# Norms of query features and latents from compact sums, and latents stored by two engines

## The reference, cut to what matters

```
z = rmsnorm(x, g_norm) @ w_in;   cq (384), ckv_raw (256), kr (32), ... = split(z)
q    = rmsnorm(cq, g_q) @ w_uq
ckv  = rmsnorm(ckv_raw, g_kv)         # returned: kv_latent of prompt and sample
k_pe = rope(kr, pos)                  # returned: k_rope of prompt and sample
mk, mv = split(rmsnorm(mem, g_mem) @ w_mem_kv)   # returned: memory keys and values
rmsnorm(x, g) = x * rsqrt(mean(x*x, last axis) + 1e-6) * g
```

## Time and profile before

| | us |
|---|---|
| median of three runs (2205.89 to 2209.16) | 2206.71 |
| profiled execution, its time | 2208.78 |
| profiled execution, its span | 2207.0 |
| TensorE busy in the span | 1908.0 |
| VectorE busy in the span | 853.1 |
| ScalarE busy in the span | 610.6 |
| TensorE's mean granted clock | 0.937 |

### The profile page before, as it was taken

How to read it: one execution, slowest core, us unless ns; L and a number is a source line. 1 busy time by engine, 2 the same in 40 slices (tenths; PEclk the granted TensorE clock), 3 DMA queues, 4 the chain that set the end, 5 groups by cost and what they waited for, 6 DMA issues and landing times. The chain is left out here.

```text
span 2207.0 us, 31815 instructions
## 1 busy us (share of the span) xinstructions
PE 1908.0 (86%) x13375; PEld 1541.7 (70%) x13375; DVE 853.1 (39%) x1487; ACT 610.6 (28%) x1153; POOL 605.5 (27%) x436
## 2 busy tenths in 40 slices
PE   6997988979997769999698888888469996999798
PEld 4643555559995346666577777777369996999776
DVE  4043455570104324444614464645541115121242
ACT  3020433342112323333222333333332223222221
POOL 0000000022213047451456000000165445445430
PEclk9998999989997999999899999999689998999899
DMA  7002000001111247561227212120143332333322
GB/s 259 0 10 61 4 7 10 1 11 44 43 39 39 76 148 235 207 184 45 72 63 198 51 47 53 46 51 11 39 137 86 86 86 57 87 86 86 128 73 77
DMA packets 186265, 167.86 MB, mean 76 GB/s; under 512 B 47228, under 2 KB 157372, under 8 KB 185756
## 3 DMA queue, kind: packets, MB, share of 16 engines
q1 hardware_dynamic: 162988, 112.89, 17.6%
q0 software_dynamic: 20592, 52.63, 8.1%
q10 hardware_dynamic: 2560, 0.56, 0.1%
HBM read 150.33 MB, written 23.01 MB: 79 GB/s over the span
## 5 line engine op out<-in xcount | busy, mean ns | idle before, releaser
L2429 PE MATMUL ps<-activations_high,weights_high 128*128 128x272 f32 x1152 | 242.8, 292 | 55.2 <-ACTq L2415 28.9
L2429 PE MATMUL ps<-activations_high,weights_low 128*128 128x272 f32 x1152 | 239.6, 290 | 0.0
L2429 PEld LDWEIGHTS ps<-activations_high,weights_high 128*128 128x128 f32 x1152 | 182.9, 191 | 57.0 <-ACT weights_high L2245 29.1
L882 DVE TENSOR_SCALAR sb<-sb 128x1536 int32<-128x1536 int32 (+3 forms) x140 | 117.9, 862 | 248.6 <-DMA sb<-in_w_in 139.4
L2383 POOL TENSOR_TENSOR weights_low<-sb 128x1536 fp32r<-128x1536 f32 x47 | 164.9, 3510 | 104.0 <-DVE sb L882 104.0
L2429 PEld LDWEIGHTS ps<-activations_high,weights_low 128*128 128x128 f32 x1152 | 182.8, 190 | 0.0
L2429 PE MATMUL ps<-activations_low,weights_high 128*128 128x272 f32 x768 | 160.4, 290 | 0.0
L2407 ACT CAST weights_high<-sb 128x1536 fp32r<-128x1536 f32 x47 | 69.5, 1479 | 313.7 <-POOL weights_low L2383 313.7
L2365 DVE TENSOR_TENSOR sb<-ps,sb 128x544 f32<-128x544 f32 (+1 forms) x48 | 34.8, 725 | 282.5 <-ACT sb L2413 263.2
L2051 PE MATMUL ps<-h_high_again,recurrence_weights_high 128*128 128x384 f32 (+1 forms) x384 | 102.2, 378 | 40.4 <-ACT sb L1894 36.4
L615 POOL TENSOR_TENSOR sb<-sb 32x1088 f32<-32x1088 f32 x8 | 19.9, 2481 | 392.4 <-ACT sb L626 392.4
(11 more groups left out here) (312 smaller groups left out, 3940.3 us busy)
## 6 DMA issues: line engine op xcount, KB each, us to landing
sb<-in_w_in SPq DMA_DIRECT2D x84, 512.0 KB, 4.0
sb<-in_w_branch SPq DMA_DIRECT2D x48, 256.0 KB, 4.2
sb<-in_x_prompt SPq DMA_DIRECT2D x16, 512.0 KB, 6.5
values_by_level<-values POOLq DMA_DIRECT2D x56, 128.0 KB, 4.4
sb<-values_by_level POOLq DMA_DIRECT2D x7, 896.0 KB, 7.6
out<-sb SPq DMA_DIRECT2D x10, 512.0 KB, 2.9
sb<-spill SPq DMA_DIRECT2D x2, 2176.0 KB, 8.0
sb<-in_w_mem_kv SPq DMA_DIRECT2D x2, 2048.0 KB, 20.6
```

What stands on the lines that cost most here:

```text
L882: return nc.vector.tensor_scalar(high.bitcast(I32), x.bitcast(I32), -4096, None, ALU.bitwise_and)
L2429: mm = nc.tensor.matmul(bank(out + s, n=HS2), w[slot][:, w0 + c, :], a[:, HS2 * s:HS2 * s + HS2], start=c == 0 and part == 0, stop=c == ch ...
```

## The change

The sums of squares change sides. A tile of 128 tokens of the squares is now the stationary operand, and the moving operand is one column of `ones`; the result is a column of 128 sums, one token on each partition. Nine tiles give nine columns in one bank (`rstd` shrinks from 1088 to 9 words a partition). Mean, root and inverse are taken of these nine columns. Then nine products a norm (`spread`) bring the inverse roots back to all partitions: the stationary operand is a column of `rstd`, repeated 128 times, and the moving operand is the identity; the results stand in three banks as `spans` reads them, and VectorE normalises with that PSUM operand.

In TensorE's list the rotary product goes ahead of `memory(0)`, `spread(1)` (latents) goes between `memory(0)` and `memory(1)`, and `spread(0)` (query features) behind `memory(1)`. In VectorE's list the rotary key goes ahead of the norms, and the query features' norm goes behind the small copies of the latents. The tiles of latents are copied by VectorE (even) and ScalarE (odd), still out of PSUM banks 6 and 7, into four SBUF buffers: tile i waits for the store of tile i-4.

```diff
-        rstd = [work.take(T) for _ in range(2)]
+        rstd = [work.take(TILES + 1) for _ in range(2)]
-        natural = work.take(2, KVL + ROPE)
+        NAT = 4
+        natural = work.take(NAT, KVL + ROPE)
...
+        token_tiles = [(i, 128 if i < TILES else TN) for i in range(TILES + 1)]
+        def keep_natural(eng, copy, i):
+            rows = token_tiles[i][1]
+            eng.wait_ge(s_nt, i + 1)
+            if i >= NAT:
+                eng.wait_ge(s_st[i % NAT], 32 * (i // NAT))
+            b = 6 + i % 2
+            copy(natural[0:rows, i % NAT, 0:KVL], bank(b, rows, 0, KVL)).then_inc(s_nt_ev[i % 2], 1)
+            copy(natural[0:rows, i % NAT, KVL:KVL + ROPE], bank(b, rows, KVL, ROPE)).then_inc(s_nt_ev[i % 2], 1)
...
             # scalar
                 for n in range(4):
                     memory(n)
+                for i in range(1, TILES + 1, 2):
+                    keep_natural(act, nc.scalar.copy, i)
...
             # vector
-                    for y, src in zip(token_pieces(rstd[k]), spans(4 * k)):
-                        ins = nc.vector.tensor_scalar(y, src, 1.0 / width, EPS, ALU.mult, ALU.add)
+                    for rows, at, n in ((128, 0, TILES), (TN, TILES, 1)):
+                        nc.vector.tensor_scalar(rstd[k][0:rows, at:at + n], bank(4 * k, rows, at, n), 1.0 / width, EPS,
+                                                ALU.mult, ALU.add).then_inc(s_mean, 1)
...
+                def normalise(k):
+                    x, chunks, width, g = norms[k]
+                    dve.wait_ge(s_rsp, 2 - k)
+                    for c in range(chunks):
+                        for y, r in zip(token_pieces(x[:, c, :]), spans(4 * k)):
+                            ins = nc.vector.scalar_tensor_tensor(y, y, g[:, c:c + 1], r, ALU.mult, ALU.mult)
+                        ins.then_inc(s_norm[k], 1)
...
             # tensor
-                        for s, (t0, tn) in enumerate(TOKEN_SPANS):
-                            mm = nc.tensor.matmul(bank(4 * k + s, n=tn), ones, sq[(3 * k + c) % 2][:, t0:t0 + tn],
-                                                  start=c == 0, stop=c == chunks - 1)
+                        for i, rows in token_tiles:
+                            mm = nc.tensor.matmul(bank(4 * k, rows, i, 1), sq[(3 * k + c) % 2][:, 128 * i:128 * i + rows],
+                                                  ones[:, 0:1], start=c == 0 and i == 0, stop=c == chunks - 1,
+                                                  skip_group_check=True)
+                def spread(k):
+                    pe.wait_ge(s_rinv, k + 1)
+                    for i, rows in token_tiles:
+                        mm = nc.tensor.matmul(bank(4 * k + i // 3, at=128 * (i % 3), n=rows),
+                                              rstd[k][0:rows, i:i + 1].to_broadcast([rows, 128]), ident[0:rows, 0:rows],
+                                              start=True, stop=True, skip_group_check=True)
+                    mm.then_inc(s_rsp, 1)
```

More of the change, by code:

```diff
@@ L323, in build @@
         s_root = sem("root_over_features")
+        s_rone = sem("roots_cleared")
+        s_rinv = sem("root_over_features_inverted")
+        s_rsp = sem("root_spread_over_partitions")
+        s_rot1 = sem("rotary_key_swapped_kept")
         s_norm = [sem(f"{x}_normalised") for x in ("query_features", "latents")]
@@ L327, in build @@
         s_nt = sem("latent_turned")
-        s_nt_ev = sem("latent_turned_evacuated")
+        s_nt_ev = [sem(f"latent_turned_evacuated_by_{x}") for x in ("vector", "scalar")]
         s_v2 = sem("vector_chain2")
-        s_st = [sem(f"latent_stored{i}") for i in range(2)]
+        s_st = [sem(f"latent_stored{i}") for i in range(NAT)]
         s_mst = sem("memory_stored")
@@ L364, in _ @@
                     rows = 128 if i < TILES else TN
-                    sp.wait_ge(s_nt_ev, 2 * i + 2)
+                    sp.wait_ge(s_nt_ev[i % 2], 2 * (i // 2) + 2)
                     if i < TILES:
@@ L369, in _ @@
                         lat, pe_ = (a[0].rearrange("b t c -> (b t) c") for a in (lat_s, rope_s))
[L370 to L373, removed]
+                    sp.dma_start(lat, natural[0:rows, i % NAT, 0:KVL]).then_inc(s_st[i % NAT], 16)
+                    sp.dma_start(pe_, natural[0:rows, i % NAT, KVL:KVL + ROPE]).then_inc(s_st[i % NAT], 16)
+                for i in range(NAT):
+                    sp.wait_ge(s_st[i], 32 * len(range(i, TILES + 1, NAT)))
                 sp.wait_ge(s_mst, 32)
@@ L399, in _ @@
                 for k in range(2):
-                    act.wait_ge(s_mean, k + 1)
+                    act.wait_ge(s_mean, 2 * k + 2)
                     nc.scalar.activation(rstd[k], rstd[k], ACT.Sqrt).then_inc(s_root, 1)
@@ L407, in _ @@
                 chain = Chain(dve, s_v2)
+                for k in range(2):
+                    nc.vector.memset(rstd[k], 1.0).then_inc(s_rone, 1)
+                dve.wait_ge(s_rone, 2)
                 for k, (x, chunks, width, g) in enumerate(norms):
                     dve.wait_ge(s_ssum, 3 * k + chunks)
-                    for y, src in zip(token_pieces(rstd[k]), spans(4 * k)):
-                        ins = nc.vector.tensor_scalar(y, src, 1.0 / width, EPS, ALU.mult, ALU.add)
-                    ins.then_inc(s_mean, 1)
@@ L413, in _ @@
-                for k, (x, chunks, width, g) in reversed(list(enumerate(norms))):
+                    for rows, at, n in ((128, 0, TILES), (TN, TILES, 1)):
+                        nc.vector.tensor_scalar(rstd[k][0:rows, at:at + n], bank(4 * k, rows, at, n), 1.0 / width, EPS,
+                                                ALU.mult, ALU.add).then_inc(s_mean, 1)
+                for k in range(2):
                     dve.wait_ge(s_root, k + 1)
[L415 to L418, removed]
@@ L419, in _ @@
-                dve.wait_ge(s_norm[1], 2)
+                    nc.vector.reciprocal(rstd[k], rstd[k]).then_inc(s_rinv, 1)
                 dve.wait_ge(s_rmm, 1)
                 dve.wait_ge(s_rot, 64)
-                for y, src, s in zip(token_pieces(kT[64:96, :]), spans(4, ROPE, 64), token_pieces(sinT[64:96, :])):
-                    ins = nc.vector.tensor_tensor(y, src, s, ALU.mult)
-                chain.link(ins)
+                swapped = (ps[64:96, 512:1536].rearrange("p (s t) -> p s t", s=2)[:, :, 0:SPAN],
+                           ps[64:96, 128:128 + T - 2 * SPAN])
@@ L426, in _ @@
+                for y, x, s in zip(token_pieces(kT[64:96, :]), swapped, token_pieces(sinT[64:96, :])):
+                    nc.vector.tensor_tensor(y, x, s, ALU.mult).then_inc(s_rot1, 1)
                 chain.link(nc.vector.tensor_tensor(krT[64:96, :], krT[64:96, :], cosT[64:96, :], ALU.mult))
+                dve.wait_ge(s_rot1, 2)
                 chain.link(nc.vector.tensor_tensor(kT[64:96, :], kT[64:96, :], krT[64:96, :], ALU.add))
+                def normalise(k):
[5 more added lines that the diff above has]
+                        ins.then_inc(s_norm[k], 1)
@@ L428, in _ @@
+                normalise(1)
+                dve.wait_ge(s_norm[1], 2)
                 chain.link(nc.vector.tensor_copy(ckvNewT, ckvT[:, :, TP:T]))
                 nc.vector.tensor_copy(kpeNewT[0:32, :], kT[64:96, TP:T]).then_inc(s_kpe, 1)
+                normalise(0)
                 dve.wait_ge(s_mk_t, 1)
[L431 to L437, removed]
+                nc.vector.tensor_copy(mkT.rearrange("p h m -> p (h m)"), ps[:, 2048:3072]).then_inc(s_mk_te, 1)
@@ L438, in _ @@
+                for i in range(0, TILES + 1, 2):
                     if i == TILES:
[L439 to L442, removed]
+                        dve.wait_ge(s_nt, i + 1)
+                        chain.link(nc.vector.tensor_copy(newNat[0:TN, :], bank(6 + i % 2, TN, 0, KVL)))
+                    keep_natural(dve, nc.vector.tensor_copy, i)
@@ L477, in memory @@
                         mm.then_inc(s_mkv, 1)
-                memory(0)
                 pe.wait_ge(s_rot, 64)
@@ L482, in _ @@
                 for s, (t0, tn) in enumerate(TOKEN_SPANS):
-                    mm = nc.tensor.matmul(bank(4 + s, ROPE, 0, tn, 64), rotc[64:96, :], krT[64:96, t0:t0 + tn],
-                                          start=True, stop=True)
+                    out = bank(1 + s, ROPE, 0, tn, 64) if s < 2 else bank(0, ROPE, 128, tn, 64)
+                    mm = nc.tensor.matmul(out, rotc[64:96, :], krT[64:96, t0:t0 + tn], start=True, stop=True)
                 mm.then_inc(s_rmm, 1)
+                memory(0)
+                pe.wait_ge(s_mean, 4)
+                spread(1)
                 memory(1)
+                pe.wait_ge(s_rot1, 2)
+                spread(0)
+                pe.wait_ge(s_norm[1], 2)
                 for h in range(HC):
                     for j in range(2):
-                        mm = nc.tensor.transpose(bank(1 + h // 2, at=(h % 2) * 256 + 128 * j, n=128),
+                        mm = nc.tensor.transpose(bank(4 + h // 2, at=(h % 2) * 256 + 128 * j, n=128),
```

(3 more changed lines are left out.)

## The result

The changed kernel takes 2224.91 us (median of four runs, 2218.84 to 2228.11) against 2207.8 for the kernel before: a ratio of 1.0075, with a 95% interval of 1.0051 to 1.0099. The ratio is taken over the executions, here that of their means (+16.5 us), while the medians lie 17.1 us apart. The kernel is slower, by 11 to 22 us; 2220 had been forecast.

A forecast was written before the change was run, and what follows sets the result against it. TensorE was taken to bound the block up to the memory values, then turn, copy and store; 7.7 + 2.0 + 2.2 + 1.6 = +13.5 us on the 2206.7 us median gave 2220 us, range 2210 to 2225.

The forecast's parts named there:

- the last rival: Block's tail: clock falls again ahead of tile 2 and nine stores queue, +3 us more, 2223 us; chance 8%.
- second term: Rotary product and memory keys begin at clock 0.50, losing 1.6 to 3.3 us; +2.0 us taken.
- The four terms: Changes on the block's path: sums +7.7, clock behind them +2.0, latents' spread +2.2, tail +1.6 us.
- What bounds: Second block: TensorE sets it up to the memory values' end, then turn, copy and store; VectorE's big inversions cost nothing.
- The sums: Sums of squares on TensorE: 90 loads at clock 0.50 throughout, 18.7 us against 10.98, +7.7 us.
- the first rival: Sums of squares: clock rises to 1.00 after 3.3 us, sums take 11.7 us; 2210.6 us in all; chance 17%.
- The clock behind them: Rotary product and memory keys after the sums start at clock 0.50; 1.6 to 3.3 us lost, +2.0 us taken.
- spread(1): Latents' spread between the memory halves: nine products, all on TensorE's path, +2.2 us.
- The tail: From the memory values' end to the next block: spread, norm, copies and tile rounds take 17.7 against 16.1 us, +1.6.

The follow-up runs named there:

- h_all: Changed kernel with sums 128 columns wide, query features' spread ahead of the memory values, nine buffers and stores of two tiles: 2210.51 us, ratio 1.0006.
- e2_early: Changed kernel with the query features' spread moved ahead of the memory values: 2221.82 us, ratio 1.0055.
- e3_fill: Changed kernel with four extra, unread products of 128x384 in TensorE's idle time ahead of the sums: 2223.54 us, one execution.
- e1_wide: Changed kernel with each product of the sums 128 columns wide instead of one: 2216.87 us, ratio 1.0027.
- e4_pairs: Changed kernel with nine buffers for the tiles of latents and stores of two tiles at a time: 2224.03 us, ratio 1.0062.
- e5_two_engines: Kernel before, norms as before, with only four buffers for the tiles of latents and odd tiles copied by ScalarE: 2207.30 us, ratio 0.9989.
- g_best: Kernel before with tiles through four PSUM banks, six buffers, ScalarE on even and VectorE on odd tiles, stores of two tiles: 2203.98 us, ratio 0.9979.

## Why the prediction was right, step by step

The forecast of 2220 us came out at 2224.91, within the range, but its +11 to +15 was too low. The outcome is nearest to the last rival, given 8%, with the longer start of its second term, 2224.5 us: the clock did fall again in the wait ahead of tile 2 (0.50 from 191 us on), the stores did queue, and the start at 0.50 was the longer one. The four terms all had the right sign.

*What bounds.* Right: TensorE sets the block up to the memory values, and the large inversions on VectorE had been free. h_all, with the inversions gone and the losses mended, is no faster than the kernel before.

*The sums.* +6.9 instead of +7.7. The price of a load at 0.50 was right: 18.98 us for the 90 in e2_early, less 0.4 for the last one's end, over 85 full widths is 0.22. In the changed kernel's profiled execution the first 1.4 us ran at 1.00. That the sums do not raise the clock was the step that carried the forecast. The row of L2146 from which it was taken could not show it, since 1.31 us of idle time stand between that row and the fall. The changed kernel's own rows show it, against the first rival: the clock falls in the sums and stays at 0.50 to their end, as in e3_fill without idle time ahead, and with 128 columns (e1_wide) it comes back.

*The clock behind them.* Too small: +3.7 (1.8 for the rotary product and 1.9 for the memory keys) instead of 2.0. I had taken a little over the length of one start at 0.50, 3.3 us, as it stood in the rows, close to the low end of my own bound. Here it lasted from 148.81 to some 156.3 us, over twice that, and half of it is lost: more than the 3.3 us at which the bound ended. The rotary product ran at 0.50 throughout, which the bound allowed for, and the memory keys for another 3.7 us. Why the start is longer than before was not tested.

*spread(1).* +2.24 for a forecast of 2.2.

*The tail.* +4.0 instead of +1.6, in part for a reason that was not named. The series of spread, norm, memory-key copy and tile 0 came as worked out (norm 4.24 for 4.05; tile 0 done 8.0 us behind the memory values). The rounds were near the upper end of what I had bounded, 1.7 us at a clock of 0.50. With them alone, in e4_pairs, the tail is +1.8. I had said that with four buffers a store has time enough to land; but a store has also to be issued, one after the other on SyncE, and 18 of them behind a late tile 0 take 8.8 us even without a long one (e3_fill): +2.4. The rest, 1.6 us, came with the one issue of 2.01, which no row of before let one expect. From the end of tile 0's copy to the next block it was 12.0 us instead of 9.6. The term had the landing time in it and not the issue, which SyncE's queue in the kernel before already shows in pairs:

```profile
175.09 0.33 SPq L370 DMA_DIRECT2D out<-sb  x1
175.47 0.43 SPq L371 DMA_DIRECT2D out<-sb  x1
```

The sum of the terms measured is 6.9 + 3.7 + 2.2 + 4.0 = 16.8 us in the block, against 13.5. That the median moved by 17.1 fits it. The profiled execution's own 10.0 is the block's 16.8 and 1.7 ahead of it, less 6.5 in the third block and 2.0 behind that.

## What to carry to other kernels

Before a product is turned so that its large operand becomes the stationary one and a single column moves, count the loads, and price them at the lower clock: here 90 loads for 45 columns of sums ran at 0.50 but for the first 1.4 us, and the products behind them paid for it too. The 14 us taken off VectorE, which waited in any case, were worth nothing here; spread, norm and copy, put in series at the block's end, were what tile 0 then waited for. At such an end look at the issuing queue as well: two stores a tile at almost half a microsecond each were the bound in e5_two_engines, whose issue has no gap from tile 0 on although two engines copy into four buffers. In the changed kernel, whose rounds were slower, the same regular issue cost only some 0.6 us.

## What had not been expected of the hardware

SyncE's one long issue: 2.01 us in the changed kernel and 2.03 in e1_wide, 1.44 in e2_early, 1.11 in h_all, where its neighbours take 0.37 to 0.48; in e3_fill, e5_two_engines and g_best there is none. In the four executions with it one packet of 0.02 MB runs on the queue of kind "instruction" in that stretch, and in the three without it none does. In e4_pairs there is such a packet and no long issue; SyncE waits for copies there. The three others have such a packet too, only earlier: within 186.83 to 187.03 us in e3_fill, ahead of its first store at 191.39, and near 160 us in e5_two_engines and g_best. That the issue waits for this packet fits the rows, but no run was made to show it, and what sets the packet's moment stays open.
